# Two transformer blocks on one core: the rows of six norms shared among three engines, first products regrouped, three low halves placed anew

## The reference

```python
def rmsnorm(x, g):
    return x * rsqrt(mean(x * x) + EPS) * g            # norms 2 and 3

def post_norm(x, sub, g, b):                           # norms 4 to 9
    y = DN_ALPHA * x + sub
    return (y - mean(y)) * rsqrt(var(y) + LN_EPS) * g + b
```

## Time and profile before

| what | value |
|---|---|
| median of 3 runs | 1381.06 us (1379.97 to 1382.18) |
| the profiled execution | 1383.32 us |
| its span | 1381.4 us |
| TensorE (PE) busy | 98% |
| VectorE (DVE) busy | 77% |
| ScalarE (ACT) busy | 47% |
| GpSimd (POOL) busy | 4% |
| mean granted TensorE clock | 0.997 |

### The profile page before, as it was taken

One profiled execution on the slowest core, in us unless ns is written; L12 is line 12 of the kernel. 1 busy time (PEld: TensorE's weight loads), 2 busy tenths in 40 slices (PEclk: granted clock), 3 DMA queues, 4 the chain that ended last, 5 costly groups with the idle time before them and its releaser, 6 DMA issues.

```text
span 1381.4 us, 22475 instructions
## 1 busy us (share of the span) xinstructions
PE 1351.6 (98%) x8881; PEld 1223.2 (89%) x8881; DVE 1058.9 (77%) x1560; ACT 643.2 (47%) x802; POOL 61.8 (4%) x72
## 2 busy tenths in 40 slices
PE   8999999999999999999999999999999999999997
PEld 7989988898899998999889998889999887899996
DVE  6978697777877778668887778767777867877777
ACT  5565644333344344553344435344344468543432
POOL 2000040000000000000110000000000000100000
PEclk9999999999999999999999999999999999999999
DMA  9533756776667767555556656767565530566661
GB/s 298 184 125 120 239 174 191 247 228 207 208 210 241 266 211 228 183 186 182 173 197 205 205 199 226 239 206 232 195 209 189 178 114 20 183 214 207 204 198 61
DMA packets 191664, 268.69 MB, mean 195 GB/s; under 512 B 5773, under 2 KB 164657, under 8 KB 191328
## 3 DMA queue, kind: packets, MB, share of 16 engines
q1 hardware_dynamic: 186574, 250.08, 55.7%
q0 software_dynamic: 4368, 16.44, 3.7%
q10 hardware_dynamic: 642, 1.05, 0.3%
HBM read 262.32 MB, written 4.19 MB: 193 GB/s over the span
## 4 chain that ended last, share of the span: by engine, by line
PE 79%; DVE 13%; ACT 4%; DMA 1%; issue 1%; POOL 1%; SPq 0%; DVEq 0%; ACTq 0%
PE bank L849 78%; DVE split L2197 3%; PE bank L872 2%; DVE stats L2243 1%; DVE resid L2269 1%; DVE resid L2277 1%; DMA ring<-in_w_in 1%; ACT split L1710 1%; DVE resid L2238 1%; ACT arena L2087 1%; DVE arena L2421 1%; ACT act_out L2096 0%; DVE best L2420 0%; DVE hT L2291 0%; ACT hT L1732 0%
## 5 line engine op out<-in xcount | busy, mean ns | idle before, releaser
L849 PE MATMUL bank<-hT,split 128*128 128x512 f32 (+1 forms) x4472 | 674.1, 311 | 0.7 <-DVE split L2197 0.6
L849 PEld LDWEIGHTS bank<-hT,split 128*128 128x128 f32 x4472 | 623.6, 191 | 46.6 <-issue 3.9
L2197 DVE TENSOR_TENSOR split<-ring,split 128x2048 fp32r<-128x2048 f32 x218 | 496.9, 2281 | 198.5 <-ACT split L1710 195.3
L1710 ACT ACTIVATE split<-ring 128x2048 fp32r<-128x2048 f32 (+1 forms) x220 | 419.6, 1910 | 453.6 <-PE bank L849 443.4
L849 PE MATMUL bank<-split,hid_hi 128*128 128x512 f32 x992 | 271.2, 380 | 1.6 <-DVEq L2605 1.0
L849 PEld LDWEIGHTS bank<-split,hid_hi 128*128 128x128 f32 x992 | 183.2, 189 | 26.8 <-issue 1.9
L849 PE MATMUL bank<-split,hT 128*128 128x256 f32 (+2 forms) x1320 | 170.1, 287 | 3.5 <-DVE split L2197 1.3
L849 PEld LDWEIGHTS bank<-split,hT 128*128 128x128 f32 x1320 | 159.2, 192 | 10.8 <-issue 4.2
L849 PE MATMUL bank<-split,hid_lo 128*128 128x512 f32 x496 | 151.4, 379 | 0.0
L2544 DVE TENSOR_REDUCE act_out<-bank 128x256 f32<-128x512 f32 x188 | 128.6, 686 | 20.4 <-PE bank L849 19.9
L849 PEld LDWEIGHTS bank<-split,hid_lo 128*128 128x128 f32 x496 | 93.8, 189 | 13.1
(11 more groups left out here) (232 smaller groups left out, 875.4 us busy)
## 6 DMA issues: line engine op xcount, KB each, us to landing
ring<-in_ffn_w SPq DMA_DIRECT2D x132, 1024.0 KB, 5.3
ring<-in_w_in SPq DMA_DIRECT2D x17, 1024.0 KB, 5.9
ring<-in_w_mlp_in SPq DMA_DIRECT2D x16, 1024.0 KB, 5.9
ring<-in_w_mlp_out SPq DMA_DIRECT2D x16, 1024.0 KB, 5.0
ring<-in_sgu_w_in SPq DMA_DIRECT2D x16, 1024.0 KB, 5.4
ring<-in_sgu_w_out SPq DMA_DIRECT2D x8, 1024.0 KB, 4.9
ring<-in_kv_w SPq DMA_DIRECT2D x6, 1024.0 KB, 5.3
ring<-in_w_out SPq DMA_DIRECT2D x4, 1024.0 KB, 5.0
```

The costliest lines, as they stand in the source:

```text
L849: ins = pe.matmul(o, lhsT, rhs, start=start, stop=stop)
L1710: act.activation(halves(q if i is None else q + BODY, n)[0], ring[:, u % SLOTS, 0:n], ACT.Copy).then_inc(hi_ready, 1)
L2197: dve.tensor_tensor(lo, ring[:, u % SLOTS, 0:n], hi.bitcast(F32), ALU.subtract).then_inc(split_ready, 1)
```

## The change

- In norms 2, 3, 4, 5, 6 and 8 (`SHARED`) the quarter (0,1) is no longer made by VectorE. ScalarE centres and scales it in one pass (`scale_second_half`), GpSimd multiplies by the gain and, from norm 4 on, adds the bias (`second_half`). VectorE's passes and low parts are put in another order (its `shared_norm`): rows of (0,0), then the adds of the second block, rows of (1,0), low part of (0,1), rows of (1,1).
- `down_last` puts the transposes of (0,0) in the middle of the six held back products. The transposes of (0,1), (1,0) and (1,1) stand in a new `first_units`, which takes the place of the three old ways to multiply the first two units. It has the same 96 products, in groups by high and low parts and by halves of the width.
- ScalarE's `shared_norm` rounds the weight unit between the two quarters of block 0, computes the second deviation behind them, and loads the next table there.
- Low halves: that of (w3,1,0) goes from GpSimd to VectorE, and VectorE and ScalarE take (w1,1,0) ahead of (so,7). Of (mu,1), VectorE keeps 768 of 2048 columns and GpSimd makes the rest. Of (w3,3,0), VectorE makes 512 columns and GpSimd the rest.
- The turned tiles of the second block of rows go to banks 4 and 5.
- The last norm is written out: ScalarE centres and scales (0,0), GpSimd applies gain and bias to it, VectorE makes the other three quarters, the last of them in two parts. The stores are five; the last one, 256 columns wide, is on ScalarE's queue.

```diff
...
+SHARED = (2, 3, 4, 5, 6, 8)
+SHARED_ACC = {("n", n, 1, h): 4 + h for n in SHARED for h in range(2)}
...
-SPLITS = dict(UNITS)
-SPLIT_NAMES = list(SPLITS)
 ORDER = plan_units()
...
+def plan_split_order():
+    names = list(ORDER)
+    i = names.index(("so", 7))
+    names[i:i + 2] = names[i + 1], names[i]
+    return names
+SPLIT_NAMES = plan_split_order()
+SPLITS = {name: q for q, name in enumerate(SPLIT_NAMES)}
 GATES = 12
...
+BEGUN_BY_DVE = {("mu", 1): 3, ("w3", 3, 0): 2}
+BY_POOL = {("proj", 0)} | set(BEGUN_BY_DVE)
...
-        if name not in SPLITS:
-            continue
+    for name in SPLIT_NAMES:
...
-                    sp.dma_start(out[0, b * P:(b + 1) * P, h * 512:(h + 1) * 512],
-                                 resid[:, b, h * 512:(h + 1) * 512]).then_inc(stored, 16)
-            sp.wait_ge(stored, 16 * 4)
+            def store(b, h, q0=0, q1=2):
+                cols = slice(h * 512 + q0 * 256, h * 512 + q1 * 256)
+                sp.wait_ge(out_ready[b][h], q1 if (b, h) == (1, 1) else 1)
+                sp.dma_start(out[0, b * P:(b + 1) * P, cols], resid[:, b, cols]).then_inc(stored, 16)
+            store(0, 1)
+            store(0, 0)
+            store(1, 0)
+            store(1, 1, 0, 1)
+            sp.wait_ge(stored, 16 * 5)
...
+                if n in SHARED:
+                    add(1, 1, 1, (0,))
+                    turn_rows(n, 0, 0)
+                    add(1, 1, 1, (1,)).then_inc(unit_used, 1)
+                    return
                 for h in range(2):
                     if n < 9:
...
+            def first_units(n, units, open_place, done, hidden=None, same_bank=False):
+                half = (range(0, 4), range(4, 8))
+                o = {}
+                def some(j, b, w, a, ks):
+                    unit = parts(units[j], KT)
+                    for k in ks:
+                        ins = mm(o[j, b], act_of(a)[:, k, b * P:(b + 1) * P], two_streams(unit[w][:, k, :]),
+                                 k == 0 and (w, a) == (0, 0) and not (j and same_bank),
+                                 k == KT - 1 and (w, a) == (0, 1) and not (same_bank and not j))
+                        if k == 0:
+                            settle(ins)
+                    return ins
+                def act_of(a):
+                    return both_hT[a]
+                def by_high(j, b, h):
+                    some(j, b, 0, 0, half[h])
+                    some(j, b, 1, 0, half[h])
+                def rounded(b, h):
+                    pe.wait_ge(hT_rounded, rounded_rows(n, b, h))
+                def lows_made(b, h):
+                    tile_copied(pe, ("n", n, b, h))
+                have(units[0])
+                o[0, 0] = open_place(0, 0)
+                rounded(0, 0)
+                by_high(0, 0, 0)
+                have(units[1])
+                o[1, 0] = open_place(1, 0)
+                by_high(1, 0, 0)
+                turn_rows(n, 0, 1)
+                lows_made(0, 0)
+                some(0, 0, 0, 1, half[0])
+                some(1, 0, 0, 1, half[0])
+                rounded(0, 1)
+                by_high(0, 0, 1)
+                some(1, 0, 0, 0, half[1])
+                turn_rows(n, 1, 0)
+                some(1, 0, 1, 0, half[1])
+                lows_made(0, 1)
+                done(0, 0, some(0, 0, 0, 1, half[1]))
+                done(1, 0, some(1, 0, 0, 1, half[1]))
+                o[0, 1] = open_place(0, 1)
+                rounded(1, 0)
+                by_high(0, 1, 0)
+                turn_rows(n, 1, 1)
+                o[1, 1] = open_place(1, 1)
+                some(1, 1, 0, 0, half[0])
+                lows_made(1, 0)
+                some(0, 1, 0, 1, half[0])
+                rounded(1, 1)
+                by_high(0, 1, 1)
+                lows_made(1, 1)
+                done(0, 1, some(0, 1, 0, 1, half[1]))
+                owed[0] += 1
+                some(1, 1, 1, 0, half[0])
+                some(1, 1, 0, 1, half[0])
+                by_high(1, 1, 1)
+                some(1, 1, 0, 1, range(4, 6))
+                if hidden:
+                    hidden()
+                done(1, 1, some(1, 1, 0, 1, range(6, 8)))
+                owed[0] += 1
             def turn_rows(n, b, h):
                 rows = xn if n <= 2 else resid
-                pe.wait_ge(xn_ready, 4 * n + 2 * b + h + 1)
+                if n in SHARED and (b, h) == (0, 1):
+                    pe.wait_ge(pool_rows, shared_at(n))
+                else:
+                    pe.wait_ge(xn_ready, rows_made(n, b, h))
...
                 round_turned(n, 1)
+            def scale_second_half(n):
+                src, dst = resid[:, 0, 512:1024], (xn if n == 2 else resid)[:, 0, 512:1024]
+                if n < 4:
+                    act.wait_ge(rstd_ready, shared_at(n))
+                    act.activation(dst, src, ACT.Copy, scale=rstd[:, 0:1]).then_inc(rows_scaled, 1)
+                    return
+                link(act.activation(minus_mean[:], mv[:, 0, 0:1], ACT.Copy, scale=-1.0))
+                act.wait_ge(rstd_ready, shared_at(n))
+                link(act.activation(shift[:], minus_mean[:], ACT.Copy, scale=rstd[:, 0:1]))
+                act.activation(dst, src, ACT.Identity, bias=shift[:, 0:1], scale=rstd[:, 0:1]).then_inc(rows_scaled, 1)
+            def shared_norm(n, between, following, then=None):
+                load_table(ACT.Sqrt)
+                deviation(n, 0)
+                scale_second_half(n)
+                round_turned(n, 0, (0,))
+                round_unit(between)
+                round_turned(n, 0, (1,))
+                deviation(n, 1)
+                if following:
+                    load_table(following)
...
             round_unit(("w3", 1, 0))
-            norm(5, ("w1", 1, 1))
+            shared_norm(5, ("w1", 1, 1), ACT.Silu)
             ffn(1, (("kv", 3), ("kv", 5)))
...
             round_unit(("w3", 3, 0))
-            norm(8, ("w1", 3, 1))
+            shared_norm(8, ("w1", 3, 1), ACT.Silu)
             ffn(3, None)
             load_table(ACT.Sqrt)
             deviation(9, 0)
+            act.wait_ge(last_scale, 1)
+            r = resid[:, 0, 0:512]
+            act.activation(r, r, ACT.Identity, bias=last_shift[:, 0:1], scale=rstd[:, 0:1]).then_inc(last_centred, 1)
             deviation(9, 1)
+            act.wait_ge(out_ready[1][1], 2)
+            act.dma_start(out[0, P:2 * P, 768:1024], resid[:, 1, 768:1024]).then_inc(stored, 16)
...
+            def begin_low(name):
+                u, q = UNITS[name], SPLITS[name]
+                dve.wait_ge(hi_ready, q + 1)
+                n = BEGUN_BY_DVE[name] * UC
+                hi, lo = halves(q, n)
+                dve.tensor_tensor(lo, ring[:, u % SLOTS, 0:n], hi.bitcast(F32), ALU.subtract).then_inc(low_begun, 1)
...
+                else:
+                    if h == 0:
+                        dve.wait_ge(var_ready, NB * n + b + 1)
+                    link(dve.scalar_tensor_tensor(out=d, in0=r, scalar=mv[:, b, 0:1], in1=gain_bc[:, cols],
+                                                  op0=ALU.subtract, op1=ALU.mult))
+                if h == 0:
+                    dve.wait_ge(sd_ready, NB * n + b + 1)
+                    ins = dve.reciprocal(rstd[:, b:b + 1], sd[:, b:b + 1])
+                    if n in SHARED and b == 0:
+                        ins.then_inc(rstd_ready, 1)
+                        dve.wait_ge(rstd_ready, shared_at(n))
+                    else:
+                        link(ins)
+                if n < 4:
...
+                ins.then_inc(xn_ready, 1)
...
                         low_turned(n, 1, h)
+            def shared_norm(n):
+                add(n, 0, 0)
+                add(n, 0, 1)
+                statistics(n, 0)
+                make_rows(n, 0, 0)
+                add(n, 1, 0)
+                low_turned(n, 0, 0)
+                add(n, 1, 1)
+                statistics(n, 1)
+                make_rows(n, 1, 0)
+                low_turned(n, 0, 1)
+                make_rows(n, 1, 1)
+                for h in range(2):
...
-            for name in (("wout", 3), ("mu", 0), ("mu", 1)):
-                low_unit(name)
+            low_unit(("wout", 3))
+            low_unit(("mu", 0))
...
             low_unit(("w1", 1, 0))
-            norm(5)
+            low_unit(("so", 7))
+            low_unit(("w3", 1, 0))
+            shared_norm(5)
             low_unit(("w1", 1, 1))
             ffn(1, (("kv", 3), ("kv", 5)))
-            norm(6)
+            shared_norm(6)
...
+            begin_low(("w3", 3, 0))
...
-            norm(9)
+            add(9, 0, 0)
+            add(9, 0, 1)
+            dve.bn_aggr(mv[:, 0, :], stats[:, 0, 0:2, :]).then_inc(var_ready, 1)
+            dve.wait_ge(var_ready, NB * 9 + 1)
+            dve.wait_ge(sd_ready, NB * 9 + 1)
+            link(dve.reciprocal(rstd[:, 0:1], sd[:, 0:1]))
+            dve.scalar_tensor_tensor(out=last_shift[:, 0:1], in0=mv[:, 0, 0:1], scalar=-1.0, in1=rstd[:, 0:1],
```

(54 more changed lines are left out.)

160 lines of the change are left out of this document (86 added, 74 removed).

## The result

The changed kernel takes 1369.88 us (median of 4 runs, 1369.34 to 1370.96) where the kernel before takes 1381.12 beside it: 11.2 us less, a ratio of 0.9919 with a 95% interval of 0.9906 to 0.9931. Forecast were 1369.0 and 12.1 us. The profiled execution took 1369.35 us with a span of 1367.6, so the spans of the two profiled executions lie 13.8 us apart, 2.6 more than the medians. Two places that I don't count to the change hold 2.86 of the 13.8 us. 1.42 lie ahead of norm 2, where the order of TensorE's work is the same in all kernels here; its mark lies anywhere between 190.70 and 194.83 us in the thirteen traces.

The account below looks back on a forecast made before the run. TensorE, busy 98%, was taken to bound the kernel, with time to win where it stands in the norms and at the end. Norm stalls 11.1 plus end 1.0 gave 12.1 us: 1381.1 to 1369.0, range 1365.2 to 1374.5.

Parts of the forecast that it names:

- Part 1: TensorE's order in the six shared norms: three held-back products before the first transposes, later waits covered by 8 to 20 products.
- the residue of 0.25 us per norm: TensorE's stall assumed to remain in each of the six shared norms, out of 13.45 us for all six before.
- Part 2: Second half of the rows by ScalarE and GpSimd: hidden from TensorE, VectorE loses two passes of 0.75 in norms 4, 5, 6, 8.
- The tightest place: Second block's rows ready at 11.0 us after the first add, wanted by TensorE at 11.05; expected to cost nothing, nearly something.
- Part 3: Low halves moved between engines: norm 5's blocked pass (1.46 us) goes, norm 2's first add 1.3 us earlier, norm 8 at most 0.3.
- the forecast loss at the hidden chunk: Norm 2: chunk turned 2 products before its low part is needed instead of 6, 0.45 us more wait.
- Part 4: Kernel's end: last rows 1.0 us earlier as VectorE loses two passes; the smaller last store saves zero to 0.2.
- A: GpSimd late: at 1.6 us a pass TensorE and VectorE wait in the norms, the end gives nothing; 1371.5 to 1373.5, chance 0.15.
- B: Half the gain lost again downstream, in feed-forward waits for splits or loads: 1375 us, chance 0.09.
- C: Identity on ScalarE needs its own table, two loads of 1.28 us in each of four norms: 1377 us, chance 0.03.
- D: Slower: VectorE's adds from banks are shut out by GpSimd too, second block's rows up to 3 us later: 1384.5, chance 0.04.

Follow-up runs that it names:

- the orders alone: Kernel before with the new order of the first units, its banks and the other two engines' shared_norm lists; rows, low halves and end old: 1377.36 us, ratio 0.9969.
- the kernel without sharing: Changed kernel, but VectorE makes all four quarters of the rows in the six norms; new orders, low halves and end stay: 1372.84 us, ratio 0.9937.
- late-GpSimd run: Changed kernel with GpSimd's work on the second quarter lengthened by two passes of 256 columns in norms 4, 5, 6 and 8: 1375.2 us, ratio 0.9961.
- the run with the loads: Changed kernel with another table loaded before ScalarE's shift and wide pass and the square root's again behind, norms 4, 5, 6, 8: 1382.99 us, ratio 1.0012.
- the kernel with the old end: Changed kernel with norm 9 and stores as before: VectorE makes all rows, four stores of 512 columns: 1371.94 us, ratio 0.9928.
- both kernels that share norm 7: Changed kernel with norm 7 shared too and norm 2's hidden chunk reordered, in two tries: 1368.94 us (ratio 0.9916) and 1368.13 us (0.9902).

## Why the prediction was right

**The bound** was read rightly: TensorE stood in the norms, and 9.8 of the 13.45 us counted went. The time came out 0.9 us above the forecast 1369.0.

**Part 1.** Transposes wanted at 5.23, 8.4 and 11.05 us from the first add came at 5.23, 8.46 and 11.20; the 16 products at 6.60, forecast 6.58. The term that was too small is the residue of 0.25 us per norm. In norm 4 it is 20.80 measured less 20.27 of work (36 x 0.216 + 96 x 0.113 + 4 x 0.41) = 0.53. The gap at 549.68 is 0.28 of it and a first product of 0.30 us behind the transposes, in place of 0.216, 0.09; the rest isn't resolved. It is also there in norm 3, from which I had forecast 0.77 and got 0.47. Five norms with 0.19 to 0.30 and norm 2 with 0.06 are the whole difference of 1.28 us between the forecast 11.10 and the measured 9.82.

**Part 2.** GpSimd was forecast at 1.31 us a pass (measured 1.28) and done at 8.0 (8.2), the wide pass at 0.65 (0.81), the centring at 8.60 (8.84), the reciprocal at 10.0 (9.98). The straight line through the two GpSimd rows named gives 1.34, not 1.31, which changes nothing. What the prediction leaves unsaid is how little of VectorE's relief reaches TensorE. The kernels in a row show it: from before to the orders alone 3.9 us of the norms' 9.8, from there to the kernel without sharing (the low halves) 3.2, from there to the changed one (the sharing) 2.7. The tightest place, the second block's rows, held with 0.2 us to spare: without sharing its reciprocal comes 0.87 later and its transposes 0.66. GpSimd's rows had 0.2 us to spare too.

The Trainium skill (SBUF — State Buffer, "Who interferes with whom") has VectorE's instructions with at most one SBUF input, outside its two-port modes, free of GpSimd, and those with two in contention with a GpSimd instruction that reads SBUF. The late-GpSimd run agrees on both sides, 0.68 and 1.50 us.

**Part 3.** Norm 5 was forecast at 3.14 and gave 2.95; its blocked pass is gone and taking it back costs 1.22. In norm 2 the first add comes 2.20 us from the mark instead of 3.53, and the forecast loss at the hidden chunk came (1.4 us of wait where 1.0 stood). Norm 8's 512 columns by VectorE did nothing beside the sharing; the forecast had counted no gain for them.

**Part 4.** 1.0 and up to 0.2 forecast, 0.93 and 0.18 measured.

**Rivals.** A: not so, 1.28 us a pass. The rival had grounds: two other GpSimd passes of 512 columns (L3244) took 1.61 us on average in the same trace. At 1.6 us a pass the delay would be 0.6 us, and by the late run's slack of 0.2 TensorE would pay 0.4 of them (an estimate), inside the 0.3 to 0.9 per norm that I had. B: the feed-forward waits stay at 2.4 us in 4. C: no load stands beside Identity. I priced it at 1377, and the run with the loads took 1383; 3.2 of these 6 us are half clock in norms 4 and 6 (their 3.9 each less the 2.3 of norm 5, in its one trace), which wasn't in my sum. The Trainium skill (ScalarE: Activation LUTs, "Table sets: the hidden batching unit") lists identity among the functions in every set, and the trace agrees: no load between the square root and Identity. D: refuted by the adds, unchanged at 0.68 us.

## What to carry to other kernels

Before work is moved off a busy engine, look at what the consumer can do meanwhile: the new orders paid without the sharing, the sharing without TensorE's order cost 8 us in the norms, and only together did both pay in full. Price each part by undoing it alone, check that nothing else went with it, and count the distance between two fixed products in both traces; medians of runs can't see a part of 1 us in 1370. A wait of TensorE can be paid twice, as a wait and in clock.

## What the runs showed that I had not expected

**Half clock behind short waits.** At the end of norm 7, which isn't changed, TensorE stands 0.97 and 0.79 us ahead of the last two groups of transposes. In the trace of the kernel with the old end the 256-column products behind them then take 0.21 us instead of 0.11 (columns as above, granted clock third from the end):

```profile
1089.50:1090.60 1.10, 1.04 (x8) 0.95 (x8) 0.34 (x2) 0.95 (x3) 1.10 (x3) 0.79 0.04 15
1090.60:1093.80 3.20, 3.20 (x18) 3.06 (x17) 2.57 (x2) 2.32 (x4) 1.43 (x2) 0.54 0.99 309
```

and in the changed kernel, behind the same waits, they don't:

```profile
1089.00:1090.20 1.20, 1.14 (x12) 1.04 (x11) 0.43 (x2) 1.02 (x3) 1.20 (x3) 1.00 0.12 31
1090.20:1091.80 1.60, 1.60 (x17) 1.46 (x15) 1.60 (x2) 1.56 (x4) 1.36 (x2) 1.00 1.00 371
```

The lower of the two levels, 1.2 GHz, shows in 3 of the 11 profiled executions in which norm 7 is as before (before, old end, table loads) and costs some 1.5 us in each. Whether it comes seems chance: the code there is the same in all eleven, and neither profile of the changed kernel has it. That it is chance is argued from this, not shown. In both kernels that share norm 7 it is absent, but two profiles don't prove that sharing keeps it away.

**Restart after being shut out.** In the late-GpSimd run VectorE's blocked pass ended 0.54 us after GpSimd's pass, against 0.75 for a whole one; in the kernel before it was 0.55. What happens in the pass meanwhile no row shows.
